# Global attention's value products: three bf16 products in place of one fp32 product

## The reference

```
h = RMSNorm(x) * (1 + scale1) + shift1
[qA|kA|vA|qB|kB|vB|gA|gB] = h @ w_in
oA = softmax(qA kA^T) vA      all tokens of a group, 8 heads of 64, 2 kv heads, blocks of 128 queries
oB = the same within |i-j| <= 128, with bias and sink
x  = x + gate1 * ((sigmoid(gA) * (oA @ w_branch_a) + sigmoid(gB) * (oB @ w_branch_b)) @ w_out)
x  = x + gate2 * mixture of 16 experts (expert choice) of RMSNorm(x) * (1 + scale2) + shift2
```

## Time and profile before

| | us |
|---|---|
| median of 3 runs | 2337.54 (2336.62 to 2340.11) |
| profiled execution | 2339.17 |
| its span in the profile | 2337.3 |
| TensorE busy | 2267.6 (97%) |
| VectorE busy | 1618.8 (69%) |
| ScalarE busy | 1224.1 (52%) |
| GpSimd busy | 1090.9 (47%) |

### The profile page before, as it was taken

The page is one execution under the profiler, slowest core; times in us unless marked ns, Lnnn a source line. Parts: engine busy times, 40 slices in busy tenths (PEclk is TensorE's granted clock), DMA queues, the critical chain, the costliest instruction groups (busy, mean ns, idle before and its releaser), DMA issues.

```text
span 2337.3 us, 55038 instructions
## 1 busy us (share of the span) xinstructions
PE 2267.6 (97%) x23919; PEld 1664.6 (71%) x24026; DVE 1618.8 (69%) x1973; ACT 1224.1 (52%) x1568; POOL 1090.9 (47%) x711
## 2 busy tenths in 40 slices
PE   8998999999999999989999999999999999999996
PEld 3554676664444458688888888888888888888874
DVE  4776666583222456777877878788878878787875
ACT  4333666593111236556655665665566555656554
POOL 0000111132332215556666677667667766766742
PEclk9999999999999999999999999999999999999998
DMA  9102201503222345578899999989998998999996
GB/s 340 40 22 73 55 2 38 181 2 91 55 54 63 103 159 163 185 278 288 303 334 341 316 338 329 324 316 342 331 320 319 340 336 308 342 335 320 323 326 239
DMA packets 252439, 524.24 MB, mean 224 GB/s; under 512 B 8411, under 2 KB 57676, under 8 KB 252076
## 3 DMA queue, kind: packets, MB, share of 16 engines
q1 hardware_dynamic: 241692, 488.51, 59.5%
q0 software_dynamic: 10512, 32.25, 4.7%
HBM read 492.42 MB, written 28.31 MB: 223 GB/s over the span
## 4 chain that ended last, share of the span: by engine, by line
PE 84%; DMA 4%; DVE 3%; POOL 3%; issue 3%; ACT 2%; SPq 0%; DVEq 0%; POOLq 0%; ACTq 0%
PE ps L1858 23%; PE ps L1859 22%; PE ps L1857 22%; PE ps L2041 3%; PE ps L2253 3%; PE ps L2053 3%; PE ps L1918 3%; DMA acc_sample<-arena,sidx_s 2%; PE ps L1953 1%; DVE arena L1392 1%; ACT arena L1087 1%; DMA arena<-w_in 1%; PE ps L1991 1%; POOL spare L837 1%; ACT arena L974 1%
## 5 line engine op out<-in xcount | busy, mean ns | idle before, releaser
L1858 PE MATMUL ps<-arena 128*128 128x160 bf16 (+4 forms) x5617 | 1390.5, 267 | 9.0 <-issue 3.2
L1859 PE MATMUL ps<-arena 128*128 128x160 bf16 (+4 forms) x5620 | 1391.6, 267 | 0.4
L1857 PE MATMUL ps<-arena 128*128 128x160 bf16 (+4 forms) x5528 | 1357.2, 265 | 9.2 <-POOL arena L858 5.3
L1392 DVE TENSOR_TENSOR arena<-arena 128x2048 bf16<-128x2048 f32 x379 | 912.0, 2410 | 219.9 <-ACT arena L974 215.1
L974 ACT ACTIVATE arena<-arena 128x2048 bf16<-128x2048 f32 x384 | 727.1, 1905 | 227.9 <-PE ps L1859 178.6
L1857 PEld LDWEIGHTS ps<-arena 128*128 128x128 bf16 x5624 | 550.7, 98 | 160.3 <-issue 21.0
L1859 PEld LDWEIGHTS ps<-arena 128*128 128x128 bf16 x5624 | 550.7, 98 | 154.8 <-issue 2.5
L1858 PEld LDWEIGHTS ps<-arena 128*128 128x128 bf16 x5624 | 550.7, 98 | 140.6 <-issue 0.3
L868 POOL TENSOR_TENSOR arena<-arena 128x320 bf16<-128x320 f32 x128 | 258.7, 2021 | 10.0
L865 POOL TENSOR_TENSOR arena<-arena,ones 128x320 bf16<-128x320 f32 x128 | 185.8, 1452 | 142.3 <-DVE arena L1735 142.0
L1245 ACT ACTIVATE arena<-ps 128x160 f32<-128x160 f32 x256 | 77.9, 304 | 295.4 <-PE ps L1859 295.3
(11 more groups left out here) (263 smaller groups left out, 2213.8 us busy)
## 6 DMA issues: line engine op xcount, KB each, us to landing
arena<-w_e_gate SPq DMA_DIRECT2D x64, 2048.0 KB, 9.1
arena<-w_e_up SPq DMA_DIRECT2D x64, 2048.0 KB, 9.8
arena<-w_e_down SPq DMA_DIRECT2D x64, 2048.0 KB, 9.9
arena<-w_ada SPq DMA_DIRECT2D x12, 2048.0 KB, 9.3
arena<-w_in SPq DMA_DIRECT2D x30, 512.0 KB, 5.3
arena<-x_sample SPq DMA_DIRECT2D x16, 512.0 KB, 3.7
arena<-w_in SPq DMA_DIRECT2D x3, 2048.0 KB, 16.9
arena<-w_out SPq DMA_DIRECT2D x2, 2048.0 KB, 9.2
```

Of the source, the lines that this page charges most:

```text
L1392: ve.tensor_tensor(lo, stage_half(kind, a), hi, ALU.subtract).then_inc(lo_done, 1)
L1857: pe.matmul(out, w_hi, x_hi, start=start, stop=False)
L1858: pe.matmul(out, w_hi, x_lo, start=False, stop=False)
L1859: return pe.matmul(out, w_lo, x_hi, start=False, stop=stop)
```

## The change

In the global branch the value products become three bf16 products. The values are split while tiles are projected: ScalarE copies them to `raw` with the keys, and GpSimd makes a high and a low part of each tile (`VA`). Of the turned probabilities, kept as fp32 in `PTs`, the high part is not written at all: TensorE reads the upper two bytes of each word as bf16 (`upper`, every second half-word). The low part, probability minus that, goes to `PL`: for n = 1 of a wide item it is made by VectorE behind its copy, for every other piece by GpSimd. `PV` waits for them (`low_at`). The window branch keeps fp32 values (`VB`). Since `PL` lies where the first merge weights are loaded, `mw_load(0)` moves behind the last global values, between the loads of chunks 9 and 10.

```diff
@@ -291,7 +291,7 @@
         hT = at(26112, 2, KD, P)
         qT = half_words(10240, NT, 2 * NPAIR, 2 * P)
         kT = half_words(20480, 2, 2, TOK)
-        V = at(23552, 2, NT, P)
+        VA, VB = half_words(23552, NT, 2 * P), at(24832, NT, P)
         R3, R4 = 28160, 40448
         RH = 29184
         ada_slot = {c: o for c, o in enumerate([0, 4096, 10240, 14336])}
@@ -314,6 +314,7 @@
         PbN = at(41472, 2, 2, 256)
         PbB = at(41472, 8, 386).rearrange("p (i h) w -> p i h w", h=2)
         PTs = [at(37376, 2, 2, 8, P), at(44560, 2, 2, 3, P)]
+        PU, PL = half_words(37376, 4, 8, 2 * P), half_words(26112, 4, 8, P)
         on = [at(45568, 2, 512), at(39424, 2, 512)]
         rb = [at(23040, 512), at(40448, 512)]
         biasm = at(46592, 8, 386)
@@ -417,6 +418,7 @@
         xn_ready = sem("xn_ready")
         g_done, g_free = sem("g_done"), [sem(f"g_free{n}") for n in range(5)]
         q_in, q_sqrt, qf_ready, q_high = sem("q_in"), sem("q_sqrt"), sem("qf_ready"), sem("q_high")
+        v_in, v_high, v_split, p_low = sem("v_in"), sem("v_high"), sem("v_split"), [sem("p_low_vec"), sem("p_low_pool")]
         s_done, nm_ready, e_done = sem("s_done"), sem("nm_ready"), sem("e_done")
         b_done = sem("b_done")
         pv_done, o_norm, o_split = sem("pv_done"), sem("o_norm"), sem("o_split")
@@ -563,6 +565,39 @@
 
         n_add = lambda i: i - first_b + 1
 
+
+        freed = {}
+        uses = [0, 0, 0]
+        for n, (s, _) in enumerate(jobs):
+            if s[0] == "br":
+                freed[n] = (brow_ready, s[1] + 1)
+            elif s[0] == "AR":
+                freed[n] = (modrow_ready, s[1] + 1)
+            elif s[0] == "AC":
+                freed[n] = (mod_ready, s[1] + 1)
+            elif s[0] == "GT":
+                freed[n] = (gt_ready, s[1] + 1)
+            elif s[0] == "OT":
+                freed[n] = (rb_copied, s[1] + 1)
+            elif s[0] in ("IS", "I"):
+                freed[n] = (idx_ready, jobs[n][1] + (1 if s[0] == "IS" else 3))
+            else:
+                uses[n % 3] += 1
+                freed[n] = (t_free[n % 3], uses[n % 3])
+
+        def upper(i, hh, z):
+
+            return PU[:, i % 2 * 2 + hh, z, 1::2]
+
+        def low_vec(i, n):
+            return n_parts(items[i]) == 4 and n == 1
+
+        lows, low_at = [0, 0], {}
+        for x in steps:
+            if x[0] == "TE" and items[x[1]][0] == 0:
+                q = 0 if low_vec(*x[1:]) else 1
+                lows[q] += 1
+                low_at[x[1:]] = (p_low[q], lows[q])
 
         block = ctx.enter_context(nc.Block())
 
@@ -623,11 +658,14 @@
             sp.wait_ge(t_done, job_at[(("Q", NT - 1), 2)] + 1)
             skew = bass.AP(tensor=brow_d, offset=127, ap=[[8 * RELW - 1, P], [RELW, 8], [1, 384]])
             sp.dma_start(biasm[:, :, 1:385], skew).then_inc(bias_in, 16)
-            mw_load(0)
             for c in range(6, 12):
 
                 sp.wait_ge(t_done, job_at[(("AR", c - 2), 0)] + 1)
                 sp.dma_start(at(ada_slot[c], KD, 512), ada_v[:, :, c * 512:(c + 1) * 512]).then_inc(ada_in[4 + c % 2], 16)
+                if c == 9:
+
+                    sp.wait_ge(pv_done, first_b)
+                    mw_load(0)
 
             for m in range(1, KD):
 
@@ -767,6 +805,25 @@
 
             for s in steps:
                 k = s[0]
+                if k == "G":
+
+                    t = s[1]
+                    if t == 0:
+                        gp.wait_ge(bias_out, 16)
+                    gp.wait_ge(v_in, t + 1)
+                    gp.tensor_tensor(VA[:, t, 0:P], raw[:, 640:768], ones[:], ALU.mult).then_inc(v_high, 1)
+                    gp.wait_ge(v_high, t + 1)
+                    gp.tensor_tensor(VA[:, t, P:2 * P], raw[:, 640:768], VA[:, t, 0:P], ALU.subtract).then_inc(v_split, 1)
+                if k == "TE" and items[s[1]][0] == 0 and not low_vec(*s[1:]):
+
+                    i, n = s[1:]
+                    hh, a = piece(i, n)
+                    gp.wait_ge(*freed[job_at[(("T", i, n), 0)]])
+                    if i >= 2:
+                        gp.wait_ge(pv_done, i - 1)
+                    z = slice(a, min(a + 4, len(items[i][3])))
+                    gp.tensor_tensor(PL[:, i % 2 * 2 + hh, z], PTs[0][:, i % 2, hh, z], upper(i, hh, z), ALU.subtract)\
+                        .then_inc(p_low[1], 1)
                 if k == "RB":
                     g = s[1]
                     if g:
@@ -1023,16 +1080,17 @@
                         ac.wait_ge(g_done, 3 * t + c + 1)
                         n = 3 * t + c
                         b = ps[:, n % 5]
-                        if c:
-                            v0 = 128 if c == 1 else 384
+                        if c == 1 and t:
+                            ac.wait_ge(v_split, t)
+                        if c == 2:
                             if t == 0:
                                 ac.wait_ge(bias_out, 16)
-                            ac.activation(V[:, c - 1, t, :], b[:, v0:v0 + P], ACT.Copy)
+                            ac.activation(VB[:, t, :], b[:, 384:512], ACT.Copy)
 
                         if c == 0:
                             ins = ac.activation(raw[:, 0:512], b, ACT.Copy)
                         elif c == 1:
-                            ac.activation(raw[:, 512:640], b[:, 0:P], ACT.Copy)
+                            ac.activation(raw[:, 512:768], b[:, 0:2 * P], ACT.Copy).then_inc(v_in, 1)
                             ins = ac.activation(rawB[:, :, 0, :], b[:, 256:512].rearrange("p (j d) -> p j d", j=NPAIR),
                                                 ACT.Copy)
                         else:
@@ -1547,6 +1605,11 @@
                     z = min(4, len(items[i][3]) - a)
                     ve.tensor_copy(PTs[0][:, i % 2, hh, a:a + z, :], b[:, 0:z * P].rearrange("p (n q) -> p n q", n=z))\
                         .then_inc(free, 1)
+                    if low_vec(i, n):
+                        z = slice(a, a + z)
+                        ve.wait_ge(*freed[job_at[(("T", i, n), 0)]])
+                        ve.tensor_tensor(PL[:, i % 2 * 2 + hh, z], PTs[0][:, i % 2, hh, z], upper(i, hh, z), ALU.subtract)\
+                            .then_inc(p_low[0], 1)
                 if k == "RB":
                     g = s[1]
                     ve.wait_ge(e_done, 2 * NPAIR * (g + 1))
@@ -1823,25 +1886,6 @@
 
         @block.tensor
         def _(pe):
-
-            freed = {}
-            uses = [0, 0, 0]
-            for n, (s, _) in enumerate(jobs):
-                if s[0] == "br":
-                    freed[n] = (brow_ready, s[1] + 1)
-                elif s[0] == "AR":
-                    freed[n] = (modrow_ready, s[1] + 1)
-                elif s[0] == "AC":
-                    freed[n] = (mod_ready, s[1] + 1)
-                elif s[0] == "GT":
-                    freed[n] = (gt_ready, s[1] + 1)
-                elif s[0] == "OT":
-                    freed[n] = (rb_copied, s[1] + 1)
-                elif s[0] in ("IS", "I"):
-                    freed[n] = (idx_ready, jobs[n][1] + (1 if s[0] == "IS" else 3))
-                else:
-                    uses[n % 3] += 1
-                    freed[n] = (t_free[n % 3], uses[n % 3])
 
             def bank(s, n=0):
 
@@ -2048,11 +2092,23 @@
                         pe.wait_ge(*freed[job_at[(("T", i, n), 0)]])
                     if i % NPAIR == 0 and i:
                         pe.wait_ge(o_norm, i // NPAIR)
+                    if i == 0:
+                        pe.wait_ge(v_split, NT)
+                    if br == 0:
+                        for n in range(n_parts(items[i])):
+                            pe.wait_ge(*low_at[(i, n)])
                     for n, kt in enumerate(kts):
-                        for hh in range(2):
-                            ins = pe.matmul(ps[hh * 64:hh * 64 + 64, 4, j * P:(j + 1) * P],
-                                            V[:, br, kt, hh * 64:hh * 64 + 64], PTs[br][:, i % 2, hh, n, :],
-                                            start=(n == 0), stop=(n == len(kts) - 1), tile_position=(0, 64 * hh))
+                        passes = ((0, 0), (1, 0), (0, 1)) if br == 0 else ((0, 0),)
+                        for x, (u, v) in enumerate(passes):
+                            for hh in range(2):
+                                d = slice(u * P + hh * 64, u * P + hh * 64 + 64)
+                                if br:
+                                    w, m = VB[:, kt, d], PTs[1][:, i % 2, hh, n, :]
+                                else:
+                                    w, m = VA[:, kt, d], PL[:, i % 2 * 2 + hh, n] if v else upper(i, hh, n)
+                                ins = pe.matmul(ps[hh * 64:hh * 64 + 64, 4, j * P:(j + 1) * P], w, m,
+                                                start=n + x == 0, stop=n == len(kts) - 1 and x == len(passes) - 1,
+                                                tile_position=(0, 64 * hh))
                     ins.then_inc(pv_done, 1)
```

## The result

Before 2338.3 us (2336.6 to 2340.1), after 2361.9 (2360.4 to 2366.4), four executions each: a ratio of 1.0104, 95% interval 1.0086 to 1.0121. The change costs 23.6 us where 3.8 were forecast, and the time lies above the range. The profiled execution spans 2358.5 us. A set is a number of executions taken together with some of the kernel before. In two later sets the changed kernel stood at 1.0061 (1.0046 to 1.0077), 14.5 and 15.8 us over before. The 8 to 10 us between come, as far as the traces show, from a stall outside the changed part that only some executions have. So there are two errors to explain.

The account below looks back on a forecast made before the run. TensorE is busy 97%, but leads the 5.15 us scores loop by only 0.20 us per item. Terms +2.3 + 1.5 + 2.2 - 2.0 - 0.2 = +3.8 us give 2341.4; range 2335 to 2358, the forecast's own 2336 to 2346.

Parts of the forecast that it names:

- the price of VectorE's new subtract: Wide items, VectorE's queue: one 128x512 subtract each, charged 0.65 to 0.7 us; bounds 0.35 and 1.0.
- the term for the company of both engines: Wide items: GpSimd's late subtract overlaps VectorE's; some lateness, a few hundredths on VectorE's side, together +1.5 us.
- up to 0.7 us more: Wide items: lengthening of GpSimd's fourth-piece subtract beside VectorE's new one, 0.1 to 0.3 us late in some iterations.
- each kind of iteration: Wide items: plain 5.15 us in place of 5.35, RB +0.33 to 5.68, NM +0.38 to 6.67; group 22.65.
- The values' gain: TensorE, wide items: values take 1.43 us in place of 1.90, a gain of 0.47 per item.
- the paired loads: TensorE's values: two weight loads of a pair start together; rival of unpaired loads 2368 us, chance 0.04.
- the 5.15 loop: Wide items: loop of scores, maxima, exponentials, next scores takes 5.15 us, so TensorE's savings beyond 0.20 are lost.
- the wait at "PV 5": Last narrow items: values of item 5 wait for GpSimd's low parts behind "NM 0", +2.2 us.
- GpSimd too slow: Rival, wide items: GpSimd's subtract takes 1.5 us or more reading every second half-word; +10 to +25, say 2354; chance 0.16.
- Items 34 to 40: End of the global branch: TensorE is ahead in four iterations, so the 0.47 is real there; -2.0 us.
- The moved load: First merge weights, now ahead of modulation row 10's load on SP's queue: taken 0, bound 5.0 us.
- the projections' -0.2: End of the projections: ScalarE makes one copy fewer per tile, -0.2 us.

Follow-up runs that it names:

- psum_low: Changed kernel with VectorE's subtract taking its first operand from the PSUM bank, not from its SBUF copy; 2339.1 us, 1.0003 of before.
- after_again: The changed kernel with no edit, run again in a later set; 2351.6 us, 1.0061 of before.
- pool_all: Changed kernel with all four low parts of a wide item made by GpSimd, none by VectorE; 2336.8 us, 0.9996 of before.
- pool_nm_mw: pool_all with GpSimd splitting finished outputs behind the next item's low parts and first merge weights loaded behind the last modulation chunk; 2335.7 us, 0.9994 of before.
- no_pool_low: Changed kernel without GpSimd's low parts in wide items, high part multiplied in their place; VectorE's subtract stays; 2345.8 us, 1.0034 of before.
- best: As pool_nm_mw, but only the narrow groups' output splitting is held back, wide groups in their old place; 2332.1 us, 0.9968 of before.

## Why the prediction was wrong

**The step that failed is the price of VectorE's new subtract**: "With the wait for its own copy I charge 0.65 to 0.7", and with it the sentence on its company, "a few hundredths on VectorE's: together +1.5 us". Undisturbed it takes 0.69 (psum_low), right as charged. Disturbed it takes 1.20, above the 1.0 given as bound. It is disturbed by that much in three iterations of four, 3 x 0.51 = 1.5 us of the 1.55 by which the group of the changed kernel exceeds that of psum_low. Over the whole kernel the two are 12.5 us apart (2351.6 and 2339.1), where the term for the company of both engines was +1.5. The rows for it were at hand: GpSimd's 1.04 grown to 2.97 beside VectorE's subtracts. The forecast priced that meeting on GpSimd's side alone, where there is time to spare, and not on VectorE's, where there is none. Its "up to 0.7 us more" for GpSimd was 0.45 and cost nothing.

**What held.** The arithmetic around the failed term can be checked on psum_low, where that term has its forecast size. The forecast reckoned an iteration from maxima to maxima; in psum_low these start on VectorE at (maxima only)

```profile
300.85 2.36 DVE L1587 TENSOR_REDUCE nm<-ps 128x1 f32<-128x1024 f32 x2
307.49 2.35 DVE L1587 TENSOR_REDUCE nm<-ps 128x1 f32<-128x1024 f32 x2
312.63 2.35 DVE L1587 TENSOR_REDUCE nm<-ps 128x1 f32<-128x1024 f32 x2
318.27 2.34 DVE L1587 TENSOR_REDUCE nm<-ps 128x1 f32<-128x1024 f32 x2
```

and the next at 323.41. That is 6.64, 5.14, 5.64 and 5.14 against 6.67, 5.15, 5.68 and 5.15, and a group of 22.56 against 22.65: each kind of iteration was right. (From scores to scores the same group reads 5.49, 5.15, 5.63 and 6.29, as late maxima delay the scores of the next item.) The time, 2339.1, lies inside the forecast's own range (2336 to 2346), but that is in part luck: psum_low is 8.3 us behind before where the merge starts (547.77 against 539.47), and 5.3 of them come back by the end of the span (2340.3 against 2337.3), for which the forecast had no term. The values' gain (0.40 for 0.47), the paired loads (48 in 1.41 us from 315.57 in the changed kernel, where one takes 0.11 on average), the 5.15 loop as a floor and the wait at "PV 5" (2.17 for 2.2, plus the clock) were right. The rival "GpSimd too slow" named 2354, close to what the kernel takes without the stall, but with the wrong mechanism: its subtract takes 1.04 us on every second half-word, and no value of the wide groups waits for it.

**The other terms**, scores starts of after_again against before. First wide scores 246.63 against 243.80: +2.8 (forecast 2.2). At the third wide item 259.31 against 255.24: +4.1; of it 3.0 is the order of "NM" (258.84 in pool_all, 255.88 in pool_nm_mw). Six groups of 1.77 or 1.78 bring +14.8 at 404.01. Items 34 to 40 gave back 0.4 at most (forecast -2.0; in pool_all, with no subtract on VectorE, about -1.5). The moved load, taken as 0 with a bound of 5.0, costs 4.4 in one step (466.07 to 475.82, 9.75 against 5.35) for a wait of 2.7 us; its row's own matmuls take 3.60 instead of 1.92, at a granted clock of 0.50. That makes +18.4 where the merge starts (557.88 against 539.47). Some 4 of it come back before the experts: TensorE's waits for nothing that the profile shows (2.40 to 0.43) and for GpSimd's first expert operand (5.27 to 3.66) shrink by 3.6; that they shrink because TensorE comes later is argued, not shown. 14.5 are left, and the stall brings the first set to about 23.6.

Of the projections' -0.2 nothing can be said: the first profile of the changed kernel is 1.6 us ahead at its first scores, the second 0.0, so that is more than the term.

**Why the stall falls on VectorE in some executions and on GpSimd in others** stays open. In all thirteen traces without the wait VectorE's addition is seen to start first, by 0.74 to 0.79 us.

## What to carry to other kernels

Before giving VectorE and GpSimd two-operand work in the same stretch, list where they meet and charge the meeting to the engine that the loop waits for. Here a meeting cost 0.51 us beside instructions of 1.04 us in three iterations of four, 0.98 beside one of 1.16 in no_pool_low, and 8.7 in the output stage where the stall struck. Taking one operand from PSUM (psum_low, the subtract at 0.69 us), or giving all such work to the engine with time to spare (pool_all), removed it; either alone brought the kernel back to its time before (1.0003 and 0.9996). Only the second together with the new place of the load and the new order of the narrow groups' "NM" made the change worth having (best, at 2332.1, is 0.3% faster than before and 19.5 us faster than after_again). And a wait put in ahead of a busy stretch cost more than itself where the clock fell with it: 2.2 us became some 3 (granted clock 0.57 over the scores behind it), and 2.7 became 4.4 (0.50).

## What the runs showed of the hardware

Two instructions with two SBUF operands, one on VectorE and one on GpSimd, didn't share in attention: VectorE's subtract of 0.69 us, when it is held, ends 0.54 us after GpSimd's instruction does, be it that 0.67 us of that were left (at 314.46 in the changed kernel) or 1.13 (in no_pool_low). With the first operand of VectorE's subtract in PSUM (psum_low) its 1.20 falls to 0.69. What in the chip holds them apart no trace shows. From the measured 1.04 of GpSimd's subtract and this 0.54, an estimate for a subtract of VectorE that begins together with one of GpSimd is 1.04 + 0.54 = 1.58 us, where the forecast had 1.0 as its bound. The meeting in no_pool_low fits the same sum: 1.16 + 0.54 = 1.70, and 1.68 was measured for one that begins 0.03 later.

In the output stage the meeting reads otherwise. VectorE's 128x1024 addition that begins 0.74 us ahead of GpSimd's conversion by the trace is held in some executions not for one instruction but for two of GpSimd in a row (992.07 + 8.11 = 1000.18; it ends at 1001.27), 9.94 us in place of 1.22. There it wasn't the one that started first by the trace that went ahead, and the hold was longer than one instruction.
